# Stick-breaking heads scored two at a time, the FFN's sums one weight unit later, the rotated key spread by DMA

## The reference, cut to what matters

```
for i in range(DEPTH):                       # 4
    h = rmsnorm(x, attn_norm[i])
    x = x + mixer[i % 3](h)                  # stick-breaking, MLA, window, stick-breaking
    x = x + (silu(h2 @ w_gate) * (h2 @ w_up)) @ w_down      # h2 = rmsnorm(x, ffn_norm[i]); hidden 2816

stick_breaking: 16 heads of 64, scale 1/8
    z = q @ k.T * scale;  valid = key_pos < query_pos
    log_keep = where(valid, log_sigmoid(-z), 0)
    after = reverse_cumsum(log_keep) - log_keep           # over the keys behind this one
    att = where(valid, exp(log_sigmoid(z) + after), 0);   o = att @ v

MLA: 16 heads; logits = q_nope . k_nope + q_rope . k_rope, and k_rope (32 wide) is the same for all heads
```

## Time and profile before

| | |
|---|---|
| median of 3 runs | 1259.92 us (1258.98 to 1260.55) |
| profiled execution, its own time | 1260.52 us |
| its span from first to last instruction | 1258.6 us |
| PE busy, PEld busy | 96%, 90% of the span |
| DVE, ACT, POOL busy | 60%, 49%, 21% |
| chain that ended last | PE 80%, POOL 9%, DVE 5%, ACT 4% |
| mean granted TensorE clock | 0.985 of 2.4 GHz |
| HBM | 159 GB/s over the span |

### The profile page before, as it was taken

One profiled execution on the slowest core, in us unless ns is written; L12 is line 12 of the kernel. 1 busy time (PEld: TensorE's weight loads), 2 busy tenths in 40 slices (PEclk: granted clock), 3 DMA queues, 4 the chain that ended last, 5 costly groups with the idle time before them and its releaser, 6 DMA issues.

```text
span 1258.6 us, 21368 instructions
## 1 busy us (share of the span) xinstructions
PE 1214.1 (96%) x8914; PEld 1137.0 (90%) x8914; DVE 759.9 (60%) x861; ACT 616.3 (49%) x827; POOL 265.6 (21%) x276
## 2 busy tenths in 40 slices
PE   8999899999989989999999989999999998999997
PEld 6988899998988889999899889999889888999985
DVE  7676665555587466555547556555556666655543
ACT  6687444443345544444346644444346774444431
POOL 4132511011132251101111241101111325110121
PEclk9999899999999999999999989999999998999998
DMA  8325655454533155455442245555553234554540
GB/s 312 131 101 126 185 177 189 172 201 174 192 115 122 44 182 178 171 197 185 183 168 102 101 159 178 177 190 193 177 171 129 101 111 158 187 182 170 199 167 34
DMA packets 29865, 201.06 MB, mean 160 GB/s; under 512 B 3488, under 2 KB 3616, under 8 KB 6352
## 3 DMA queue, kind: packets, MB, share of 16 engines
q1 hardware_dynamic: 28800, 197.41, 44.1%
q0 software_dynamic: 352, 1.31, 0.7%
q10 hardware_dynamic: 624, 1.04, 0.2%
HBM read 197.91 MB, written 1.84 MB: 159 GB/s over the span
## 4 chain that ended last, share of the span: by engine, by line
PE 80%; POOL 9%; DVE 5%; ACT 4%; issue 1%; DMA 0%; DVEq 0%; POOLq 0%; ACTq 0%
PE bank L1169 17%; PE bank L1170 17%; PE bank L1171 17%; PE bank L1177 13%; PE bank L1178 7%; PE bank L1163 4%; POOL qk_parts L389 3%; POOL sq L316 3%; DVE w_lo L758 2%; POOL sq_sum L320 1%; PE bank L1245 1%; ACT qk_parts L501 1%; ACT w_hi L448 1%; ACT qk_parts L505 1%; DVE x_split L773 1%
## 5 line engine op out<-in xcount | busy, mean ns | idle before, releaser
L758 DVE TENSOR_TENSOR w_lo<-raw,w_hi 128x2048 fp32r<-128x2048 f32 x183 | 428.7, 2343 | 283.9 <-ACT w_hi L448 283.8
L1169 PE MATMUL bank<-x_split,w_hi 128*128 128x256 f32 x1792 | 513.9, 287 | 0.0
L1170 PE MATMUL bank<-x_split,w_hi 128*128 128x256 f32 x1792 | 510.0, 285 | 0.0
L1171 PE MATMUL bank<-x_split,w_lo 128*128 128x256 f32 x1792 | 509.7, 284 | 0.0
L448 ACT ACTIVATE w_hi<-raw 128x2048 fp32r<-128x2048 f32 x183 | 349.3, 1909 | 194.9 <-PE bank L1171 131.8
L1169 PEld LDWEIGHTS bank<-x_split,w_hi 128*128 128x128 f32 x1792 | 347.2, 194 | 4.0 <-issue 2.4
L1170 PEld LDWEIGHTS bank<-x_split,w_hi 128*128 128x128 f32 x1792 | 347.1, 194 | 0.5
L1171 PEld LDWEIGHTS bank<-x_split,w_lo 128*128 128x128 f32 x1792 | 347.0, 194 | 0.0
L1177 PE MATMUL bank<-hid_split,w_hi 128*128 128x512 f32 x704 | 248.9, 399 | 0.0
L1178 PE MATMUL bank<-hid_split,w_lo 128*128 128x256 f32 x704 | 197.7, 281 | 0.0
L1177 PEld LDWEIGHTS bank<-hid_split,w_hi 128*128 128x128 f32 x704 | 132.3, 188 | 32.9
(11 more groups left out here) (166 smaller groups left out, 1187.8 us busy)
## 6 DMA issues: line engine op xcount, KB each, us to landing
raw<-w SPq DMA_DIRECT2D x183, 1024.0 KB, 4.8
raw<-w SPq DMA_DIRECT2D x8, 256.0 KB, 6.5
x<-x_in SPq DMA_DIRECT2D x2, 512.0 KB, 5.4
raw<-w SPq DMA_DIRECT2D x2, 512.0 KB, 8.4
out<-x SPq DMA_DIRECT2D x4, 256.0 KB, 2.6
rel_scratch<-rel_lut POOLq DMA_DIRECT2D x1, 768.0 KB, 11.3
rel_bias<-rel_scratch POOLq DMA_DIRECT2D x2, 256.0 KB, 7.9
scratch<-consts ACTq DMA_DIRECT2D x1, 416.0 KB, 3.5
```

Of the source, the lines that this page charges most:

```text
L758: dve.tensor_tensor(w_lo[slot][:, :], raw[slot][:, :], w_hi[slot][:, :].bitcast(FP32), ALU.subtract).then_inc(lo_done, 1)
L1169: pe.matmul(dst, wh, xh, start=first, stop=False, skip_group_check=True)
L1170: pe.matmul(dst, wh, xl, start=False, stop=False, skip_group_check=True)
L1171: return pe.matmul(dst, wl, xh, start=False, stop=last, skip_group_check=True)
```

## The change

Four things are changed.

1. **Scores in pairs.** The two heads' queries lie side by side in `q_split`, each with its own 64 rows filled and the other 64 rows zero (POOL sets the zeros once a layer, `query_zeros`). One matmul with the whole 128-row key tile then gives both heads' scores. Banks 0 and 1, and 2 and 3, are declared as one 1024-column tensor each (`scores_bank`): columns 0 to 511 hold the early keys of both heads, 512 to 767 the late keys. The three products are high by high, low key by high query, high key by low query. ACT's and DVE's steps cover 768 columns at once. ACT makes one key and two query copies, DVE the low queries, POOL none.
2. **Sums in fp32r.** `neg_one` is rounded like `neg_tri` (both in `neg_sums`), and the sum over the late tile is taken from the high and the low softplus.
3. **Later sums, earlier splits.** In SwiGLU `model_sums` stands behind up 0, and both splits of unit b + 3 stand at the stage's start. In stick-breaking the splits stand one pair earlier on ACT and DVE.
4. **The rotated key by DMA.** ACT waits for `krope_new` and issues one DMA that writes the 15 copies (64 partitions x 15 x 1 KB); POOL's copies are gone, and PE waits for the whole DMA.

```diff
-        qk_parts = placed("qk_parts", [P, 5, SEQ], FP32R, 8 * HEADS * SEQ + 8 * D)
+        q_split = placed("q_split", [P, 2, 2, SEQ], FP32R, 4 * KT * SEQ)
+        k_split = placed("k_split", [P, 2, SEQ], FP32R, 4 * HEADS * SEQ + 4 * KT * SEQ)
...
-        soft_split = sb("soft_split", [P, 2, 2, 384], FP32R)
-        neg_tri = sb("neg_tri", [P, P], FP32R)
+        soft_split = sb("soft_split", [P, 2, 768], FP32R)
+        neg_sums = sb("neg_sums", [P, 2 * P], FP32R)
+        neg_tri, neg_one = neg_sums[:, 0:P], neg_sums[:, P:2 * P]
...
-        bank = [ctx.enter_context(nc.psum_tensor(f"bank{i}", [P, 512], FP32)) for i in range(8)]
+        scores_bank = [ctx.enter_context(nc.psum_tensor(f"scores{i}", [P, 1024], FP32)) for i in range(2)]
+        bank = [scores_bank[i // 2][:, 512 * (i % 2):512 * (i % 2) + 512] for i in range(4)]
...
-                    pool.tensor_copy(k_all[HD:P, first:last, :],
-                                     k_all[HD:P, 0:1, :].to_broadcast([HD, last - first, SEQ])).then_inc(m.kfill, 1)
-                    pool.wait_ge(m.kfill, part + 1)
...
+                for h in range(2):
+                    if h:
+                        pool.wait_ge(mixer[i].q_zero, 1)
+                    pool.memset(q_split[others(h), :, h, :].bitcast(FP32), 0.0).then_inc(mixer[i].q_zero, 1)
...
+                    act.wait_ge(m.qk_new, 2 * p + 2)
+                    act.activation(k_split[:, 0, :], k_all[:, p, :], ACT.Copy).then_inc(m.k_hi, 1)
                     for h in range(2):
...
-                    for rows in (own, others):
-                        for h in range(2):
-                            act.activation(query_parts[h][rows(h), :], q_all[own(h), p, :],
-                                           ACT.Copy).then_inc(m.q_hi, 1)
+                        act.activation(q_split[own(h), 0, h, :], q_all[own(h), p, :], ACT.Copy).then_inc(m.q_hi, 1)
...
+                    e, z = buf(0, 768), scores_bank[p % 2][:, 0:768]
+                    act.wait_ge(m.z, p + 1)
+                    t = step(act.activation(e, z, ACT.Abs))
+                    act.wait_ge(act_step, t)
+                    t = step(act.activation(e, e, ACT.Exp, scale=-1.0))
+                    act.wait_ge(act_step, t)
+                    act.activation(e, e, ACT.Ln, bias=1.0).then_inc(m.ln, 1)
...
+                    act.wait_ge(m.sums, p + 1)
+                    act.activation(buf(2, 768), scores_bank[p % 2][:, 0:768], ACT.Exp).then_inc(m.att, 1)
...
-                        split(b + 7 + p)
                     if p < KT - 1:
+                        split(b + 8 + p)
                         qk_hi(p + 1)
...
+                act.wait_ge(m.krope_new, 1)
+                act.dma_start(k_all[HD:P, 1:HEADS, :],
+                              k_all[HD:P, 0:1, :].to_broadcast([HD, HEADS - 1, SEQ])).then_inc(m.kfill, 16)
                 split(b + 5)
...
+                split(b + 3)
                 first_guess(norm, n + 1, 0, SEQ + TOKEN_SUMS[n])
...
-                    split(b + 2 * c + 3)
+                    if c:
+                        split(b + 2 * c + 3)
                     split(b + 2 * c + 4)
...
+                def qk_low(p):
+                    dve.wait_ge(m.k_hi, p + 1)
+                    dve.tensor_tensor(k_split[:, 1, :], k_all[:, p, :], k_split[:, 0, :].bitcast(FP32),
+                                      ALU.subtract).then_inc(m.k_lo, 1)
                     for h in range(2):
...
+                        dve.wait_ge(m.q_hi, 2 * p + h + 1)
+                        dve.tensor_tensor(q_split[own(h), 1, h, :], q_all[own(h), p, :],
+                                          q_split[own(h), 0, h, :].bitcast(FP32), ALU.subtract).then_inc(m.q_lo, 1)
...
+                    split(b + 7 + p)
+                    dve.wait_ge(m.ln, p + 1)
+                    for dst in (sp_hi, buf(1, 768)):
+                        dve.scalar_tensor_tensor(dst, scores_bank[p % 2][:, 0:768], 0.0, buf(0, 768),
+                                                 ALU.max, ALU.add).then_inc(m.softplus, 1)
...
+                    dve.wait_ge(m.softplus, 2 * p + 2)
+                    dve.tensor_tensor(sp_lo, buf(1, 768), sp_hi.bitcast(FP32), ALU.subtract).then_inc(m.sp_lo, 1)
...
+                split(b + 3)
                 model_rstd(n)
...
+                    early, late = score_banks(p)
+                    mask = head_blocks(mask_b[:, 0:512])[:, :, 0, :]
+                    pe.matmul(head_blocks(early)[:, :, 0, :], ident_b[:, :], mask, start=True, stop=False,
+                              skip_group_check=True)
+                    pe.matmul(late, ident_b[:, :], mask, start=True, stop=False, skip_group_check=True)
...
+                    for key_low, query_low in ((0, 0), (1, 0), (0, 1)):
+                        if query_low:
+                            pe.wait_ge(m.q_lo, 2 * p + 2)
+                        elif key_low:
+                            pe.wait_ge(m.k_lo, p + 1)
+                        else:
+                            pe.wait_ge(m.q_hi, 2 * p + 2)
+                            pe.wait_ge(m.k_hi, p + 1)
+                        kk, qq = k_split[:, key_low, :], q_split[:, query_low, :, :]
+                        pe.matmul(early, kk[:, 0:P], qq.rearrange("p h s -> p (h s)"), start=False, stop=query_low == 1,
                                   skip_group_check=True)
-                        pe.wait_ge(m.q_lo, 2 * p + h + 1)
-                        r = own(h)
-                        pe.matmul(z[:, 0:SEQ], kk[r, 0:P], ql[r, :], start=False, stop=False, skip_group_check=True)
-                        pe.matmul(z[:, SEQ:384], kk[r, P:SEQ], ql[r, P:SEQ], start=False, stop=True,
-                                  skip_group_check=True).then_inc(m.z, 1)
+                        last = pe.matmul(late, kk[:, P:SEQ], qq[:, :, P:SEQ], start=False, stop=query_low == 1,
+                                         skip_group_check=True)
+                    last.then_inc(m.z, 1)
...
+                    for low, done, count in ((0, m.softplus, 2 * p + 2), (1, m.sp_lo, p + 1)):
+                        pe.wait_ge(done, count)
+                        sp = soft_split[:, low, :]
+                        pe.matmul(early, neg_tri, sp[:, 0:512], start=False, stop=False, skip_group_check=True)
+                        pe.matmul(late, neg_tri, sp[:, 512:768], start=False, stop=low == 1, skip_group_check=True)
+                        last = pe.matmul(head_blocks(early)[:, :, 1, :], neg_one, sp[:, 512:768], start=False,
+                                         stop=low == 1, skip_group_check=True)
+                    last.then_inc(m.sums, 1)
...
+                    pe.wait_ge(m.att, p + 1)
+                    at = buf(2, 768)
...
-                    pe.wait_ge(m.kfill, h // 8 + 1)
+                    pe.wait_ge(m.kfill, 16)
...
-                    if c == 0:
-                        model_sums(n)
                     if c >= 2:
                         pe.wait_ge(f.u_new, past + c - 1)
                     two_tiles(b + 2 * c + 1, UP_BANKS[c % 2], x_tile)
+                    if c == 0:
+                        model_sums(n)
```

More of the change, by code:

```diff
@@ L190, in others, with head_blocks @@
             return own(1 - h)
[L192 to L198 removed]
+        def head_blocks(v):
+            return v.rearrange("p (h b q) -> p h b q", h=2, b=2)
         def window_q(r):
@@ L417, in _ @@
                 if i % 3 == 0:
[L418 to L419 removed]
+                    query_zeros(i)
                 if i == 0:
@@ L1280, in qk, with score_banks @@
                     part(b + 4 + p, 4 + p % 2, x_tile, tiles)
+                def score_banks(p):
+                    return bank[2 * (p % 2)], bank[2 * (p % 2) + 1][:, 0:SEQ]
                 def logits(p):
-                    pe.wait_ge(m.qk_new, 2 * p + 2)
-                    for h in range(2):
-                        for first in (0, SEQ):
-                            pe.matmul(bank[2 * (p % 2) + h][:, first:first + P], ident_b[:, :],
-                                      sb_mask[:, first:first + P], start=first == 0, stop=False, skip_group_check=True)
```

104 lines of the change are left out of this document (23 added, 81 removed).

## The result

| | before | after |
|---|---|---|
| median | 1260.24 us (4 runs, 1258.98 to 1261.05) | 1215.2 us (4 runs, 1215.03 to 1215.23) |
| ratio, 95% interval | | 0.9643, 0.9626 to 0.966 |
| span of the profiled execution | 1258.6 us | 1213.1 us |
| mean granted TensorE clock | 0.985 | 0.998 |

A forecast was written before the change was run, and what follows sets the result against it. PE, working 96% of the span, was taken to bound the kernel. Terms of 24.9 + 3.9 + 19.8 = 48.6 us off the profiled 1260.5 us gave 1211.9, forecast as 1211 us, range 1205 to 1224.

The forecast's parts named there:

- Term A: SwiGLU's sums behind up 0: 15.6 us of waits for squares and 9.3 us of lower clock go, 24.9 us.
- 2.1 us of cover: SwiGLU, layer 0: up 0 runs to 152.0, squares are ready at 149.9, so PE no longer waits before the sums.
- Term C: MLA's rotated key by DMA: wait for `ms` shrinks from 3.6 to 1.4, lower clock gone; 3.9 us, bounds 1.7 and 4.4.
- The clock in MLA: Behind the shortened wait for `ms`, the lower clock was expected not to come, worth 1.7 us.
- Term B: Stick-breaking pairs: 10.7 us from cheaper matmuls, 9.5 from low-query waits, less 0.4; 19.8 us, bounds 4 and 21.
- the slower rival: Stick-breaking: reads over two banks take twice as long, low queries come 1.9 us too late per pair; 1265 us, chance 0.02.
- the surcharge that stays: Stick-breaking: matmul couples behind a wait cost as much extra as before; 1222 us or so, chance 0.1.
- The clock came back everywhere: Rival it answers: idle stretches go, but the lower clock appears elsewhere in the same stages; 1222 us, chance 0.05.
- the score chain was not late: Rival it answers: stick-breaking steps over both heads come late, 0.7 us of waiting in 14 pairs; 1221 us, chance 0.16.
- the wait for the sums didn't move to another place in full: Rival it answers: SwiGLU split late at up 0 or gate 2, half the sums' gain lost; 1224 us, chance 0.04.
- the DMA landed 9 us ahead of its use: Rival it answers: MLA key's DMA lands some 5 us late in traffic with the weights; 1216 us, chance 0.03.
- The forecast's own case: Whole kernel: all three terms come as forecast, 1211 us with range 1206 to 1217; chance 0.6.

The follow-up runs named there:

- sums_alone: Kernel before with only SwiGLU's part: sums behind up 0, unit b + 3 split early on ACT and DVE; 1237.53 us.
- experiments 1 and 5: First: changed kernel with SwiGLU's sums ahead of up 0 again, 1246.07 us. Second: changed kernel with DVE's early split behind the mean square, 1213.67 us.
- filler_before_sums, experiment 3: Kernel before with 28 matmuls, written to a bank nothing reads, ahead of SwiGLU's sums in each layer; 1252.33 us.
- pairs_alone: Kernel before with the stick-breaking heads in pairs and nothing else; 1241.99 us.
- pool_key_copies: Changed kernel with POOL's two copies of the rotated key again and no DMA; 1219.23 us.
- Experiment 6: Changed kernel with ACT's and DVE's splits of unit b + 3 back at their old places, sums still behind up 0; 1229.57 us.
- experiment 8: Changed kernel with the two low queries of each pair moved from DVE to POOL; 1246.36 us.
- sums_back: Changed kernel with only the place of SwiGLU's sums undone, ahead of up 0 again; 1246.07 us.

## Why the prediction came out as it did

*Term A, the sums: 24.9 forecast, 23.5 measured alone.* By PE's starts in sums_alone the four gate and up stages are 23.4 us shorter, of which 15.6 - 0.7 = 14.9 are waits and 8.5 the clock; MLA's stretch gives 0.4 more (below) and the start of the kernel takes 0.4 back. The mechanism and its two halves were right. The clock's half was 9.3 in the sum: 10 x (1 - clock) says a little more than PE's starts give back, as also in MLA, 1.7 against 1.5. One step was wrong: "the squares are ready at 149.9: no wait is left before the sums, 2.1 us of cover". The change itself moved them. "The early split of unit b + 3 ... takes ACT and DVE 1.92 + 2.29 us from the end of gate 0: hidden" is true for PE, but on DVE it stands beside POOL's last operations, and these took 2 us longer (experiments 1 and 5). In layer 0 of the changed kernel the squares end at 140.01 + 2.67 = 142.68, and PE starts on them at 142.73. The cover was zero, not 2.1, and in layer 2 below zero. The rows that would have told it were there: the earlier trace rows show DVE slow beside POOL, and POOL's last two operations ahead of the sums before show it the other way round, the first beside the split of 146.29, the second behind its end:

```profile
146.51 2.54 POOL L316 TENSOR_TENSOR sq<-x 128x256 f32<-128x256 f32 x1
149.13 0.72 POOL L318 TENSOR_TENSOR ss<-sq_sum,sq 128x256 f32<-128x256 f32 x1
```

I costed the hidden split on its own engine and not on its neighbour's.

*Term C, the key: 3.9 forecast, 3.2 alone (3.1 by stages, as in the changed kernel), 4.4 when undone in the changed kernel.* The prediction had the wait shrink to 1.4; it shrank to 0.85, as DVE's low latents also ran faster (1.24 us for the couple, 2.70 beside the copies). The DMA landed after 7.7 us where I took 14.1 from the earlier trace rows, at 351.9 for a need at 361.2. Against that stands the wait of 0.88 us for `q_all`, which I didn't see: PE arrives so much earlier that `queries(3)`, which stands on DVE behind two heads' maxima, is late. It also appears in sums_alone, where the key is still copied but the clock stays up. So it hangs on PE's pace and not on the DMA.

*The clock in MLA.* "I expect the lower clock not to come, 1.7 more, since its like is seen behind waits of 3.6 us and not of 0.8": the lower clock did not come, with 1.00 behind the waits of 0.85 and 0.88 us. But that it always stands behind a wait of 3.6 us did not hold. The wait of 3.60 us is the same in five kernels, and the clock behind it is not. In sums_alone it stayed up:

```profile
361.00:371.00 10.00, 7.75 (x59) 7.49 (x60) 9.58 (x15) 6.17 (x7) 0.00 (x0) 1.00 0.37 125
```

while before lost 1.7 us, filler_before_sums 1.7 (0.80 and 0.86 over two stretches of five microseconds), pairs_alone 1.7 (0.66 over five) and pool_key_copies 2.45. Experiment 6 has the same within one run: four waits of 2.6 us, a lower clock behind three. And in experiment 8 waits of only 1.5 to 2.0 us brought it in four of 14 cases. The Trainium skill, "TensorE: Matmul & The Clock Gate", section "Part 1: The HAM clock gate", says that the window in which the chip looks at PE's activity is free-running and doesn't start anew with the kernel. What a given wait costs would then depend on when it falls. The values fit that, but no run here moved one wait through time to test it, so this cause is not shown. The 1.7 us that term C counted thus hang partly on chance. In sums_alone the stretch was 0.4 us shorter with the key still copied: by PE's starts the clock gives 1.5, and 1.1 go to the new wait for `q_all` and the start behind it.

*Term B, the pairs: 19.8 forecast, 18.2 alone, 19.15 by stages.* Sums 0.96 forecast and 0.95 measured. ACT's 768 columns 0.82 and 0.81, DVE's 0.95 and 0.95: reading scores over two banks has no price, and the slower rival with it is out. The low queries end at 68.57 + 0.86 = 69.43 and PE takes them at 70.47 in the second pair, 1.0 us of cover where 0.8 was forecast, and no pair waits. The mis-sized term is masks and scores: 1.25 forecast, 1.38 measured. Couples two and three cost 0.35 and 0.36 as the earlier trace rows say. Masks and first couple together take 61.14 - 60.56 = 0.58 where 0.20 + 0.35 was forecast, and 0.09 stands between the last couple and the first values. 0.13 in 16 pairs is 2.1 us. So most of the surcharge that stays is where PE goes over from the scores to the fp32 values, and none is in each couple. The Trainium skill, "TensorE: Matmul & The Clock Gate", section "Back-to-back issue gap", has N / 2.4 + 2.5 ns as the isolated gap of a matmul; the estimate from it for a couple is 0.216 + 0.109 = 0.325 us, and the trace has 0.35, that of the earlier trace rows. Per pair PE's work went from 10.33 - 0.79 = 9.54 to 8.99, 0.55 less, 8.8 us in 16. With 9.5 of waits, and 0.6 of waits for ACT's query copies that the prediction didn't count, less 0.6 behind the last pairs, that makes 18.3, against 19.15 by stages; 0.9 stays open. The 18.2 of pairs_alone is lower for another reason, its lower clock in SwiGLU.

*The rivals.* The clock came back everywhere, the score chain was not late, the wait for the sums didn't move to another place in full, and the DMA landed 9 us ahead of its use. The forecast's own case is what happened, with 3.1 us less than its sum: by stages 1.5 in term A, 0.65 in B and 0.8 in C, each a size and not a mechanism, except for the squares that the early split delayed.

## What to carry to other kernels

When work is moved into idle time of DVE, look at what POOL is doing there, and the other way round: an operation that is free on its own engine took 2 us from its neighbour and with it the whole cover of the wait that was to be removed. A wait on PE costs more than itself: 0.26 us for its start alone (experiment 8), and behind waits of 1.5 to 6.5 us between nothing and 3.0 us of lower clock (10 x 0.30 in sums_back). Work that fills most of it gives the clock back, even if it computes nothing (experiment 3). When PE got faster by 4%, fixed orders on the other engines that just sufficed became the next waits; a list of them by place (here 0.85, 0.88 and 0.72 us) is the next change.

## What the runs showed of the hardware

- A POOL operation on 256 columns takes 0.74 us alone and 2.67 beside a DVE split of 2.29; a DVE split takes 3.98 beside POOL copies. It goes both ways.
- Behind the same wait of 3.60 us the clock was 1.00 in sums_alone, 0.65 to 0.66 over five to seven microseconds in pool_key_copies and pairs_alone. Behind four equal waits of 2.6 us in late_both_splits it was 0.83 over ten microseconds three times and 1.00 once.
- A wait of 1.53 us between score matmuls made a pair 1.79 us longer at a clock of 1.00 (10.78 against 8.99).
- Reads of 768 columns over two PSUM banks cost no more than the sum by columns: ACT 0.81 us, DVE 0.95.
- A DMA from one 64 x 256 tile to 15 copies of it inside SBUF, 960 KB in pieces of 1 KB, landed in 7.7 us.
- One plain fp32 matmul of 256 columns costs 0.43 us where one of fp32r costs 0.12.
